# Reordering three places of a four-layer transformer kernel: the first weight units, the memory attention, and the entry of the last feed-forward layer

## What is computed

```python
x = x + 0.5 * swiglu(rms_norm(x, ffn1_norm[l]), ...)
...                                           # mixer: sparse and stick-breaking attention
x = x + memory_cross_attention(rms_norm(x, mem_x_norm[l]), rms_norm(mem, mem_kv_norm[l]), ...)
x = x + 0.5 * swiglu(rms_norm(x, ffn2_norm[l]), ffn2_wg[l], ffn2_wu[l], ffn2_wd[l])

def memory_cross_attention(h, mem_n, wq, wk, wv, wo, g_q, g_k):
    q = rms_norm((h @ wq).reshape(B, T, MEM_HEADS, HEAD_DIM), g_q)   # 4 heads of 64
    s = jnp.einsum('bqhd,bkhd->bhqk', q, k) * HEAD_DIM ** -0.5       # 256 memory rows
    o = jnp.einsum('bhqk,bkhd->bqhd', softmax(s), v)
    return o @ wo

def swiglu(h, wg, wu, wd):                                           # 2816 hidden columns
    return (jax.nn.silu(h @ wg) * (h @ wu)) @ wd
```

## Time and profile before

| what | value |
|---|---|
| median of three executions | 1222.87 us |
| profiled execution, its own time | 1222.6 us |
| span of the trace | 1220.8 us |
| TensorE busy | 1208.5 us, 99% |
| VectorE busy | 714.3 us, 59% |
| ScalarE busy | 594.3 us, 49% |
| GpSimd busy | 59.8 us, 5% |
| mean granted TensorE clock | 0.999 |

### The profile page before, as it was taken

How to read it: one execution, slowest core, us unless ns; L and a number is a source line. 1 busy time by engine, 2 the same in 40 slices (tenths; PEclk the granted TensorE clock), 3 DMA queues, 4 the chain that set the end, 5 groups by cost and what they waited for, 6 DMA issues and landing times.

```text
span 1220.8 us, 15359 instructions
## 1 busy us (share of the span) xinstructions
PE 1208.5 (99%) x6189; PEld 1006.6 (82%) x6189; DVE 714.3 (59%) x966; ACT 594.3 (49%) x802; POOL 59.8 (5%) x101
## 2 busy tenths in 40 slices
PE   8999999999999999999999999999999998999998
PEld 6888888888889988888888888888997786888887
DVE  5666565554476766555447655456588747654452
ACT  6744454444354455444435544434548746543341
POOL 0100010000000000000004100000020001000000
PEclk9999999999999999999999999999999999999999
DMA  7744546544545444654453745453551222655530
GB/s 267 285 151 171 213 174 240 176 168 174 207 138 190 142 144 181 241 193 175 165 191 122 289 175 207 161 222 107 206 178 66 97 87 94 229 200 192 207 138 35
DMA packets 34687, 213.56 MB, mean 175 GB/s; under 512 B 4665, under 2 KB 6841, under 8 KB 10041
## 3 DMA queue, kind: packets, MB, share of 16 engines
q1 hardware_dynamic: 34617, 212.59, 48.3%
HBM read 211.53 MB, written 1.05 MB: 174 GB/s over the span
## 4 chain that ended last, share of the span: by engine, by line
PE 96%; DVE 2%; ACT 1%; DMA 0%; issue 0%; SPq 0%; POOL 0%; DVEq 0%; ACTq 0%; POOLq 0%
PE ps L320 29%; PE ps L322 28%; PE ps L321 28%; PE ps L326 4%; PE ps L806 2%; PE ps L765 1%; DVE wlo L1460 1%; DMA raw<-in_w_v 0%; PE ps L641 0%; ACT whi L1023 0%; DVE tmp L1478 0%; PE ps L623 0%; ACT xThi L1044 0%; ACT junk L1047 0%; PE ps L643 0%
## 5 line engine op out<-in xcount | busy, mean ns | idle before, releaser
L1460 DVE TENSOR_TENSOR wlo<-raw,whi 128x2048 fp32r<-128x2048 f32 (+2 forms) x200 | 440.5, 2236 | 113.2 <-ACT whi L1023 112.8
L1023 ACT ACTIVATE whi<-raw 128x2048 fp32r<-128x2048 f32 (+2 forms) x200 | 365.2, 1871 | 44.0 <-DMA raw<-in_w_gu 12.5
L320 PE MATMUL ps<-whi,xThi 128*128 128x512 f32 (+2 forms) x960 | 374.1, 390 | 4.6 <-DVE wlo L1460 2.8
L322 PE MATMUL ps<-whi,xTlo 128*128 128x512 f32 (+2 forms) x960 | 371.6, 387 | 0.0
L321 PE MATMUL ps<-wlo,xThi 128*128 128x512 f32 (+2 forms) x960 | 371.0, 386 | 0.0
L320 PEld LDWEIGHTS ps<-whi,xThi 128*128 128x128 f32 x960 | 180.7, 188 | 44.1 <-DVE wlo L1460 4.3
L1139 ACT ACTIVATE f_sil<-ps,stats 128x256 f32<-128x256 f32 x88 | 41.6, 473 | 359.0 <-PE ps L322 358.3
L322 PEld LDWEIGHTS ps<-whi,xTlo 128*128 128x128 f32 x960 | 180.5, 188 | 36.7
L321 PEld LDWEIGHTS ps<-wlo,xThi 128*128 128x128 f32 x960 | 180.8, 188 | 35.4
L1583 DVE SCALAR_TENSOR_TENSOR f_hid<-ps,stats,f_sil 128x256 f32<-128x256 f32 x88 | 42.4, 482 | 257.4 <-ACT f_sil L1139 257.2
L320 PE MATMUL ps<-whi,f_hThi 128*128 128x512 f32 x352 | 144.9, 412 | 0.0
(11 more groups left out here) (302 smaller groups left out, 1268.6 us busy)
## 6 DMA issues: line engine op xcount, KB each, us to landing
raw<-in_w_gu SPq DMA_DIRECT2D x88, 1024.0 KB, 5.8
raw<-in_w_dn SPq DMA_DIRECT2D x44, 1024.0 KB, 6.6
raw<-in_w_u SPq DMA_DIRECT2D x8, 1024.0 KB, 5.1
raw<-in_w_ao SPq DMA_DIRECT2D x8, 1024.0 KB, 6.5
raw<-in_w_v SPq DMA_DIRECT2D x6, 1024.0 KB, 6.0
raw<-in_w_bv SPq DMA_DIRECT2D x4, 1024.0 KB, 6.9
raw<-in_w_bk SPq DMA_DIRECT2D x4, 1024.0 KB, 5.6
raw<-in_w_bq SPq DMA_DIRECT2D x4, 1024.0 KB, 5.6
```

Of the source, the lines that this page charges most:

```text
L320: e.matmul(ps, a[0], b[0], start=start, stop=False)
L322: return e.matmul(ps, a[1], b[0], start=False, stop=stop)
L1023: e.activation(slots[slot_of[i]][0][:, cs], raw_cols(i, cs), ACT.Copy).then_inc(*inc("whi", i, p))
L1460: e.tensor_tensor(lo[:, cs], raw_cols(i, cs), hi[:, cs].bitcast(F32), ALU.subtract).then_inc(*inc("wlo", i, p))
```

## The change

**At the start**, ScalarE splits units 2 and 3 ahead of the token halves (0,1) and (1,1). VectorE splits unit 2 between the gain product of half (0,1) and its low part, and unit 3 in the same way at half (1,1). TensorE's order stays.

**In the memory attention** TensorE turns the softmax weights of tile 0 ahead of the queries of tile 1. It does those queries in two halves with `mix(0, 4)` between, and makes the output sums of tile 0 before the scores of tile 1, with `turn_q(1)` between the two halves. ScalarE and VectorE follow this order. VectorE takes `scores_max(1)` and the splits of units 166 on behind the gain products of `f3`'s tile 0.

**The last layer** loses `enter_last`. TensorE takes the units of chunks 0 and 1 together and projects tile 0 with both, with the tail between; tile 1 of chunk 0 follows, then `downs(0, 0)`, then the transposes of `hid` (0,1) and (1,0), then tile 1 of chunk 1. ScalarE and VectorE hold back part of `to_mem` (a generator, resumed by `next(lead)`) until after `gated(0, 0)`.

TensorE, the entry of the last layer and the memory attention:

```diff
+            def enter_lead():
+                pairs = [[take(), take()] for _ in range(2)]
+                def gate_up(c, t, kts=range(8)):
+                    project(("gu", S, c, t), GB[t], half_of(xT, t), pairs[c], kts=kts, normed=(S, t), last=t)
+                for h in range(2):
+                    e.wait_ge(*at("res", before, 0, h))
+                    turn_x(S, 0, h, XB[h])
+                gate_up(0, 0, range(0, 6))
+                ahead(tail, 1)
+                gate_up(0, 0, range(6, 8))
+                ahead(tail, 1)
+                e.wait_ge(*at("hid", S, 0, 0))
+                gate_up(1, 0, range(0, 3))
+                finish(tail)
+                gate_up(1, 0, range(3, 5))
+                for h in range(2):
+                    e.wait_ge(*at("res", before, 1, h))
+                    turn_x(S, 1, h, DB[0][h])
+                turn_hid(0, 0)
+                gate_up(1, 0, range(5, 8))
+                gate_up(0, 1)
+                dn = [take()]
+                downs(0, 0, dn)
+                for c, t in ((0, 1), (1, 0)):
+                    turn_hid(c, t)
+                gate_up(1, 1)
+                downs(0, 1, dn)
...
-            enter(S, before, tail, first)
-            for c in range(FFN_CHUNKS):
+            if lead:
+                enter_lead()
+            else:
+                enter(S, before, tail, first)
+            for c in range(2 if lead else 0, FFN_CHUNKS):
...
+            turn_p(0, XB)
             e.wait_ge(*at("mqe", 0))
-            queries(1)
-            turn_p(0, XB)
-            turn_q(1)
+            queries(1, range(0, 4))
             mix(0, 4)
+            queries(1, range(4, 8))
             wo = [take()]
+            e.wait_ge(*at("molo", 0))
+            e.wait_ge(*at("mpt", 0, 1))
+            for h in range(2):
+                if h:
+                    turn_q(1)
+                down_bank(h, XB[h], half_of(moT, 0), wo, ...)
             e.wait_ge(*at("res", "m", 1, 1))
             scores(1, DB[1])
-            e.wait_ge(*at("molo", 0))
-            e.wait_ge(*at("mpt", 0, 1))
-            for h in range(2):
-                down_bank(h, XB[h], half_of(moT, 0), wo, ...)
```

ScalarE:

```diff
             scaled_hi("g", 1, 0)
+            split(2)
             scaled_hi("g", 0, 1)
-            split()
             scaled_hi("g", 1, 1)
-            split()
...
             gated(0, 0)
+            if lead:
+                next(lead)
+                second()
+                hi(0, 0)
+                gated(1, 0)
+                at_chunk(0, False)
+                gated(0, 1)
+                hi(0, 1)
+                hi(1, 0)
+                gated(1, 1)
+                at_chunk(1, False)
...
             exps(0, XB)
-            for h in range(2):
-                scaled_hi("c", 1, h)
+            scaled_hi("c", 1, 0)
             e.wait_ge(*at("ss", "mq", 0))
             e.wait_ge(*at("res", "m", 1, 1))
             square_sum("c", 1, x[1][:, :])
-            split()
+            turned_p(0, XB)
+            scaled_hi("c", 1, 1)
+            split()
+            hi(0, 4)
             queries(1)
-            turned_p(0, XB)
             turned_q(1)
-            hi(0, 4)
+            split()
+            for h in range(2):
+                scaled_hi("f3", 0, h)
             exps(1, DB[1])
-            turned_p(1, DB[1])
-            for h in range(2):
-                scaled_hi("f3", 0, h)
-            hi(1, 1)
             e.wait_ge(*at("ss", "mq", 1))
             e.wait_ge(*at("res", "c", 0, 1))
             square_sum("f3", 0, x[0][:, :])
             split()
+            turned_p(1, DB[1])
+            yield
+            hi(1, 1)
             for h in range(2):
                 scaled_hi("f3", 1, h)
+            yield
```

VectorE:

```diff
             for t in range(2):
                 scale("g", t, 1, (XB, DB[0])[t][1], gain(0))
+                split()
                 scaled_lo("g", t, 1, xT)
-                split()
...
             gated(0, 0)
+            if lead:
+                next(lead)
+                lo(0, 0)
+                gated(1, 0)
+                at_chunk(0, False)
+                gated(0, 1)
+                lo(0, 1)
+                lo(1, 0)
+                gated(1, 1)
+                at_chunk(1, False)
...
             residual("m", 1, 1, MB[1][1])
+            weights(0)
             scaled_lo("c", 1, 0, xT)
             scale("c", 1, 1, DB[0][1], gain(7))
             scaled_lo("c", 1, 1, xT)
-            weights(0)
-            split()
+            lo(0, 4)
+            split()
+            for h in range(2):
+                residual("c", 0, h, XB[h])
             square_sums("mq", (1,), 4, scratch=squares)
-            lo(0, 4)
+            for h in range(2):
+                scale("f3", 0, h, XB[h], gain(9))
+                scaled_lo("f3", 0, h, xT)
             scores_max(1, DB[1])
-            for h in range(2):
-                residual("c", 0, h, XB[h])
+            split()
             weights(1)
-            scaled("f3", 0, XB, gain(9))
+            yield
+            split()
             lo(1, 1)
             split()
             for h in range(2):
                 residual("c", 1, h, DB[1][h])
             scaled("f3", 1, DB[0], gain(9))
+            yield
```

More of the change, by code:

```diff
@@ L500, in hook_free, with ffn @@
                 e.wait_ge(*at("kmT", 1))
-        def ffn(k, S, before, tail, hook=None, enter=enter):
+        def ffn(k, S, before, tail, hook=None, enter=enter, lead=False):
             pair = []
@@ L916, in to_mem, with queries @@
         def to_mem(rest):
-            def queries(t):
-                project(("mq", t), 0, half_of(xT, t), wq, cols=256, normed=("c", t), last=t)
+            def queries(t, kts=range(8)):
+                project(("mq", t), 0, half_of(xT, t), wq, cols=256, kts=kts, normed=("c", t), last=t)
             def turn_q(t):
@@ L964, in to_mem @@
                 turn_x("c", 1, h, DB[0][h])
+            turn_p(0, XB)
             e.wait_ge(*at("mqe", 0))
-            queries(1)
-            turn_p(0, XB)
-            turn_q(1)
+            queries(1, range(0, 4))
             mix(0, 4)
+            queries(1, range(4, 8))
             wo = [take()]
-            e.wait_ge(*at("res", "m", 1, 1))
-            scores(1, DB[1])
             e.wait_ge(*at("molo", 0))
@@ L975, in to_mem @@
             for h in range(2):
+                if h:
+                    turn_q(1)
                 down_bank(h, XB[h], half_of(moT, 0), wo, range(2), True, True, fresh=h == 0).then_inc(*inc("product", "sum", "c", 0, h))
+            e.wait_ge(*at("res", "m", 1, 1))
+            scores(1, DB[1])
             def tail():
@@ L990, in to_mem @@
             return tail()
-        def enter_last(S, before, tail, first):
-            for h in range(2):
-                e.wait_ge(*at("res", before, 0, h))
-            for h in range(2):
[L996 to L1000, removed]
-            for h in range(2):
-                e.wait_ge(*at("res", before, 1, h))
-                turn_x(S, 1, h, DB[0][h])
-            first(range(4, 8))
         tail = gmlp()
@@ L1012, in tensor @@
         tail = to_mem(mixer(tail))
-        tail = ffn(3, "f3", "c", tail, enter=enter_last)
+        tail = ffn(3, "f3", "c", tail, lead=True)
         finish(tail)
@@ L1130, in gmlp, with ffn @@
             split(2)
-        def ffn(S, at_chunk, second):
+        def ffn(S, at_chunk, second, lead=None):
             def gated(c, t):
@@ L1147, in ffn @@
             gated(0, 0)
-            second()
-            at_chunk(0, True)
-            for c in range(FFN_CHUNKS):
+            if lead:
[9 more added lines that the diff above has]
+                at_chunk(1, False)
+            else:
+                second()
+                at_chunk(0, True)
+            for c in range(2 if lead else 0, FFN_CHUNKS):
                 if c:
@@ L1386, in to_mem @@
             square_sum("c", 1, x[1][:, :])
+            turned_p(0, XB)
+            scaled_hi("c", 1, 1)
             split()
+            hi(0, 4)
             queries(1)
-            turned_p(0, XB)
             turned_q(1)
-            hi(0, 4)
-            exps(1, DB[1])
-            turned_p(1, DB[1])
+            split()
             for h in range(2):
                 scaled_hi("f3", 0, h)
-            hi(1, 1)
+            exps(1, DB[1])
             e.wait_ge(*at("ss", "mq", 1))
@@ L1448, in scalar @@
         mixer()
-        to_mem()
-        ffn("f3", chunks(1, [3, 4, *[3] * 7, 1, 0]), lambda: enter_second("f3", "c"))
+        last = to_mem()
+        next(last)
+        ffn("f3", chunks(0, [3, 4, *[3] * 7, 1, 0]), lambda: enter_second("f3", "c"), last)
     def vector(e):
@@ L1578, in gmlp, with ffn @@
             split()
-        def ffn(S, at_chunk):
+        def ffn(S, at_chunk, lead=None):
             def gated(c, t):
@@ L1971, in to_mem @@
             scaled_lo("c", 1, 1, xT)
-            weights(0)
+            lo(0, 4)
             split()
-            square_sums("mq", (1,), 4, scratch=squares)
```

(16 more changed lines are left out.)

## The result

The kernel after takes 1230.5 us (median of four, 1229.93 to 1231.37) against 1223.38 us for the one before (four, 1222.51 to 1224.52): ratio 1.0058, 95% interval 1.0041 to 1.0076. The forecast was 1231.1 us. The profiled execution took 1230.72 us with a span of 1228.9 us, 8.1 us longer than the span of before.

What follows compares the result with a forecast made beforehand. TensorE, busy 99% of the span, was taken as the bound. Start -0.1 and second place +8.3 us gave +8.2 on 1222.6, with 0.27 for the median 1231.1 us; range 1226.5 to 1234.5 us.

Steps and rivals of the forecast that it cites:

- D: Entry of the last layer: TensorE waits 2.1 us for hid (0,1), which stands behind units 169, 170 and 171.
- The start: First units' splits: 1.6 us won if the clock stays up behind the new wait, 0.1 us if it falls.
- Unit 4's wait: At the start: a new TensorE wait of 2.0 us for unit 4, until 23.6 us.
- First half of the attention: Memory attention: moved instructions fill former waits, so the transposes for f3 begin 2.4 us earlier.
- A: Entry of the last layer: TensorE waits 2.1 us between the transposes and the first gate-up matmul, for VectorE.
- C: Entry of the last layer: TensorE waits 3.8 us for unit 167, which VectorE splits behind gated(0, 0).
- B: Entry of the last layer: TensorE waits 3.0 us for unit 166, split on VectorE behind scores_max(1).
- The clock: Low clock after waits: a sure fall behind C, plus one at the start or behind D, about 1.6 us each.
- only the longest wait does: Rival: the clock falls only behind C, the start keeps full clock: +6.7 us, 1229.6 us, chance 0.14.
- The faster rival: Rival: VectorE stays ahead at units 166 and 167, so B, C and D vanish: -3.8 us, 1219.1 us, chance 0.04.

Runs made afterwards that it cites:

- e1_start_only: The kernel before with only the new start (reordered splits of units 2 and 3): 1221.68 us, ratio 0.9985.
- e10_attention_only: The kernel before with the new start and new memory attention order up to tile 1's scores, old last-layer entry and lists behind: 1224.78 us, ratio 1.0015.
- e3_unit167_first: The kernel after with VectorE's split of unit 167 moved ahead of gated(0, 0): 1227.62 us, ratio 1.0035.
- e4_hid01_early: The kernel after with gated(0, 1) behind one split in place of three on ScalarE and VectorE: 1228.76 us, ratio 1.0044.
- e5_both: The kernel after with unit 167 split ahead of gated(0, 0) and gated(0, 1) behind unit 169: 1225.3 us, ratio 1.0017.
- e6_unit166_first: The kernel after with VectorE's split of unit 166 moved ahead of scores_max(1): 1232.38 us, ratio 1.007.
- e2_late_only: The kernel after with the old start put back: 1232.34 us, ratio 1.0074.
- e9_fill_short: The kernel after with small unread matmuls on TensorE, 9 before unit 166 is needed and 11 before hid (0,0) is waited for: 1228.69 us, ratio 1.0048.
- e7_fill: The kernel after with small unread matmuls on TensorE, 12 before unit 166 is needed and 18 before hid (0,0) is waited for: 1230.1 us, ratio 1.005.

## Why the prediction was right, and where its parts were off

The direction, the place and the four waits came out as worked out from the lists: 1.83, 2.50, 2.82 and 1.74 us in the profile against the 1.8, 2.7, 3.5 and 1.8 it named. The time, 1230.5 us, is 0.6 us from the forecast. That it is so close is luck in part: the forecast counted one fall of the clock of 1.6 us, at the start or behind D, that did not come in the profiled execution, and had missed 1.4 us elsewhere. Its step of 0.229 us a matmul is the step between rows and holds, but 51.00 us over 234 instructions, which it names for it, give 0.218; the shorter transposes are among them.

- **The start.** Unit 4's wait ended at 23.36 us (23.6 in the prediction), and the clock stayed up. That case was to give 1.6 us; 1.34 us were there at the memory attention, and 1.8 us by the times of `e1_start_only`. The same lists of the start put the attention anywhere from 1010.19 to 1011.41 us in nine profiles, so these figures are good to some 0.5 us. The step that failed is "the weights of chunks 2 and 3 keep over 1 us of slack". It was true of the weights, but the gelu behind unit 8 had less.
- **First half of the attention.** 1.9 us in place of 2.4, and `e10_attention_only` shows that with the old entry behind them they are no gain at all. The prediction put this down as "won" and the waits as a loss beside it. Only the sum was right.
- **Waits A to D.** C and D are shown by `e3_unit167_first` and `e4_hid01_early`, and that neither hides the other by `e5_both`. `e6_unit166_first` shows what sets B, and that it can't be had for nothing. A is only read from the trace, where `xTlo` ends it; no run moved it.
- **The clock.** The prediction took C's fall as sure; it came in the profiles of after, `e2_late_only`, `e4_hid01_early` and `e6_unit166_first`. It counted one more for the start or for D, and in the profile of after neither came. It called all four waits longer than the 1.82 us one, but A and D, 2.1 us by its way of counting, come to about 1.8 as the trace counts, by its own remark that the trace shows waits 0.2 to 0.3 us shorter. So they were not longer than it. Taken by its falls, this execution is the rival "only the longest wait does", +6.7 us; profile against profile, 8.1 us were measured. Of the 1.4 us between, 0.3 are missing at the start and 0.5 in the first half. The other 0.6 are a term that the prediction set at nothing: "a fall behind B [is spent] mostly inside C". At the low clock TensorE reached `turn_p(1)` late, at 1032.08 us. ScalarE, which had to copy it, stood idle for 0.61 us (timeline of ScalarE, after), and the silu and `hid` moved back with it:

```profile
1032.87 1.09 ACT L1076 ACTIVATE y_PT<-ps 128x512 f32<-128x512 f32 x2 [0.61 <-PE ps L326]
1033.98 1.28 ACT L1161 ACT_TABLE_LOAD   x1
1035.27 0.47 ACT L1161 ACTIVATE f_sil<-ps,stats 128x256 f32<-128x256 f32 x1
```

  With the 0.5 us missing from the first half this gives the stretch's 9.4 us: 6.7 + 1.6 + 0.5 + 0.6. Two runs bear the 0.6 out. In `e9_fill_short`, at full clock behind B, C ended 14.14 us after A, in after 14.71. In `e5_both` against `e3_unit167_first` the same difference is 0.50 us.
- **The faster rival** asked for VectorE to be ahead of TensorE at units 166 and 167. It was not, though at unit 166 it is close to the limit that the prediction set: its split began at 1027.02 and ended at 1029.30 us, that of unit 167 began at 1036.18.

## What to carry to other kernels

Where engines run fixed lists, a reorder of the busiest engine is worth only what the other engines' lists let through. So work each list forward with the durations of the trace, and look for a piece of preparation that stands behind a result of the very work that it prepares. An early finish of one half, bought with a late start of the other, is a loan: follow the late half to its first use before you count a gain. And a wait is not priced by its length alone: moving unit 166 forward cut its wait by 1.4 us and cost 1.9 us by the medians, 1.5 in the trace.

## What the runs showed that I had not expected

The same wait did not always have the same effect on the clock, and the same fall did not always cost the same. Wait A, 1.83 us in each profile, was followed by the lower level in `e5_both`, `e7_fill` and `e9_fill_short`, and by full clock in after, `e2_late_only`, `e3_unit167_first`, `e4_hid01_early` and `e6_unit166_first`. The 1.82 us wait at the start was followed by a fall in both profiles that had it, before and `e2_late_only`, but at least 20 of the 50 other executions of before had none (mean granted clock 1.000). Nothing here tells in advance which it will be. What a fall costs depends on what TensorE meets next. Behind C nothing covered it: 1.53 us. At B it set `hid` back by 0.5 to 0.6 us. Behind A it was spent inside wait B: nothing. At the start, by the times of before with and without it, nothing that could be measured: unit 4 was ready only at about 24.6 us, 0.7 us before TensorE came to it at 25.28, so with a full clock it would have waited there for most of the time won. So a plan should follow each possible fall to the next wait. The Trainium skill, "TensorE: Matmul & The Clock Gate", section "Why this matters for your kernels", warns only of pauses longer than these; here pauses of 1.82 and 1.83 us were followed by a fall in some executions.

A float32 matmul of 128 columns outside the three-part scheme shows as two instructions of 0.12 us each in the profile (11 as 22 rows, 2.72 us, in `e9_fill_short`); a count of rows is not a count of matmuls in the program.
